# Row buffers, weight buffers and weight transfers of a mixture-of-experts stage rearranged

## The reference

```
def _merge_and_ffn(...):
    x1 = _layernorm(ALPHA * x + mix, ln1_g, ln1_b)
    ffn = _hier_moe(x1, w_group, b_group, w_expert, b_expert, w_gate_up, w_down)
    return _layernorm(ALPHA * x1 + ffn, ln2_g, ln2_b)

for e in range(N_EXPERTS):            # in _hier_moe; gate is zero but for two experts of a token
    gu = xt @ w_gate_up[e]            # 1024 x 512
    h = jax.nn.silu(gu[:, :D_EXPERT]) * gu[:, D_EXPERT:]
    y = y + gate[:, e:e + 1] * (h @ w_down[e])      # 256 x 1024
```

## Time and profile before

| what | value |
|---|---|
| median of three runs | 601.82 us |
| the profiled execution | 602.56 us |
| its span in the trace | 600.9 us |
| PE busy | 518.8 us (86%) |
| DVE, ACT, POOL busy | 373.2, 191.4, 134.0 us |
| DMA from 360 to 560 us | busy all the time, 396 to 419 GB/s |
| chain that ended last | PE 56%, DMA 26%, DVE 8%, ACT 7% |
| largest single item of the chain | loads of gate/up to arena_o, 19% |

### The profile page before, as it was taken

How to read it: one execution, slowest core, us unless ns; L and a number is a source line. 1 busy time by engine, 2 the same in 40 slices (tenths; PEclk the granted TensorE clock), 3 DMA queues, 4 the chain that set the end, 5 groups by cost and what they waited for, 6 DMA issues and landing times.

```text
span 600.9 us, 8960 instructions
## 1 busy us (share of the span) xinstructions
PE 518.8 (86%) x3296; PEld 281.0 (47%) x3296; DVE 373.2 (62%) x722; ACT 191.4 (32%) x356; POOL 134.0 (22%) x156
## 2 busy tenths in 40 slices
PE   5999999999979879899999898888887777767761
PEld 4887788874355443445556743333332222222220
DVE  1642059898933576652258666677886477666686
ACT  0100374214243644121142122444444244432340
POOL 1001054500025760000000201233323222221231
PEclk9999999999979999999999899999999899999997
DMA  9940008570606932001978599999999999999951
GB/s 302 405 155 6 1 1 331 213 269 1 279 5 230 395 116 87 2 1 59 417 290 342 180 420 406 409 396 419 415 415 411 419 418 419 415 415 418 401 193 43
DMA packets 34010, 157.95 MB, mean 263 GB/s; under 512 B 12680, under 2 KB 12680, under 8 KB 20016
## 3 DMA queue, kind: packets, MB, share of 16 engines
q1 hardware_dynamic: 20592, 127.46, 52.9%
q0 software_dynamic: 10752, 29.59, 13.0%
q10 hardware_dynamic: 2624, 0.34, 0.4%
HBM read 160.12 MB, written 21.23 MB: 302 GB/s over the span
## 4 chain that ended last, share of the span: by engine, by line
PE 56%; DMA 26%; DVE 8%; ACT 7%; issue 3%; SPq 0%; POOL 0%; DVEq 0%; POOLq 0%; ACTq 0%
DMA arena_o<-in_w_gu 19%; PE ps L489 17%; PE ps L748 8%; PE ps L962 8%; PE ps L985 4%; PE ps L651 3%; PE ps L589 2%; PE ps L635 2%; DVE arena_s L1477 2%; PE ps L672 2%; DMA first_rows<-arena_s,known 1%; DMA x_rows<-arena_s 1%; PE ps L555 1%; DMA known<-slot_table 1%; DMA slot_table<-arena_s 1%
## 5 line engine op out<-in xcount | busy, mean ns | idle before, releaser
L962 PE MATMUL ps<-arena_w,arena_s 128*64 128x512 f32 x368 | 109.2, 605 | 24.1 <-DMA arena_w<-in_w_gu 12.3
L489 PE MATMUL ps<-arena_w 128*128 128x260 f32 x416 | 94.5, 388 | 6.7 <-DMA arena_w<-in_w_in 6.2
L489 PEld LDWEIGHTS ps<-arena_w 128*128 128x128 f32 x416 | 79.7, 193 | 21.0 <-DMA arena_w<-in_w_in 6.2
L962 PEld LDWEIGHTS ps<-arena_w,arena_s 128*64 128x64 f32 x368 | 33.2, 139 | 96.9 <-issue 66.4
L985 PE MATMUL ps<-arena_w,cs 128*64 128x512 f32 x184 | 56.1, 615 | 20.8 <-ACT cs L1260 20.8
L748 PE MATMUL ps<-arena_o,arena_s 128*128 128x512 f32 x128 | 58.3, 601 | 1.6 <-DVE arena_s L1601 1.6
L962 PE MATMUL ps<-arena_o,arena_s 128*64 128x512 f32 x112 | 50.2, 595 | 0.0
L1477 DVE STREAM_TRANSPOSE arena_s<-arena_w 128x1024 f32<-128x1024 f32 x36 | 41.8, 1214 | 8.3 <-PE ps L589 8.2
L2150 POOL DMA_INDIRECT first_rows<-arena_s,known x15 | 18.0, 1202 | 113.9 <-ACT arena_s L1267 105.1
L1910 DVE TENSOR_TENSOR arena_s<-arena_s,ps 128x256 f32<-128x256 f32 x16 | 6.7, 421 | 56.5 <-ACT arena_s L1256 56.5
L985 PEld LDWEIGHTS ps<-arena_w,cs 128*64 128x64 f32 x184 | 16.0, 141 | 51.0 <-issue 30.3
(11 more groups left out here) (349 smaller groups left out, 897.3 us busy)
## 6 DMA issues: line engine op xcount, KB each, us to landing
arena_w<-in_w_gu SPq DMA_DIRECT2D x46, 1024.0 KB, 19.9
arena_w<-in_w_dn SPq DMA_DIRECT2D x23, 1024.0 KB, 19.9
arena_o<-in_w_gu SPq DMA_DIRECT2D x14, 1024.0 KB, 23.2
arena_o<-in_w_dn SPq DMA_DIRECT2D x7, 1024.0 KB, 23.8
arena_w<-in_w_in SPq DMA_DIRECT2D x13, 512.0 KB, 14.1
arena_o<-in_w_out SPq DMA_DIRECT2D x1, 4096.0 KB, 13.5
arena_s<-in_w_gu SPq DMA_DIRECT2D x4, 1024.0 KB, 8.1
arena_w<-in_xT SPq DMA_DIRECT2D x4, 520.0 KB, 6.7
```

The source lines that it names most:

```text
L489: last = mm(ps[rows, b + n, 0:HALF], lhs(k), rhs(k)[:, n * HALF:(n + 1) * HALF], start=(k == 0), stop=(k == ks - 1))
L962: last = mm(ps[64 * e:64 * e + 64, 2 + q, :], xgT[:, k, CAP * e:CAP * (e + 1)], gu_w[2 * slots + e][:, k, :], start=(k == 0), stop=(k == K ...
```

## The change

Five things change, none of them in the arithmetic but for a clamp.

The gate/up weights lie in another order in memory: both experts' first halves are one block of 2 MB, both second halves another. One transfer of 16 KB per partition takes the place of two of 8 KB per partition. A block fills one slot, so the second half of pair 2 goes to slot 4 and can be issued before the wait for the rows of pair 0.

After pair 2 the two slots in `arena_s` stay weight buffers. The pairs use three buffers in the order 0, 1, 2, 0, 1, 0, 1, 2 and again, so that pairs 8 and 9 wait for the pair two before, and others for the pair three or more before.

The room comes from the rows: `xg` is a ring of four, and the last pass of `finish` writes to `yo[n % 2]`, from where `scatter_out` sends it. So `gather_other(n)` waits until the output of pair n-2 has landed, and `gather_rows` fetches pair n+3, after `scatter_out(n-1)`.

`finish` runs one pair behind instead of two, on DVE, ACT (`root`) and POOL. The end of the program is rewritten: the last pair's own part is added after its partner's, straight from the results of PE, and five small multiplications stand between PE's `products` and `experts` of pair 15.

`residual` multiplies by weights that one pass has multiplied by ALPHA before, and clamps the rows; it has two passes as before.

```diff
+BUFFER = (0, 1, 2, 0, 1, 0, 1, 2)
+GU_SLOT = [[0, 1], [2, 3], [5, 4]]
-S_XG = [5120, 6144, 0, D, S_RT] + [S_SLOT + D * n for n in range(3)]
-S_YO = [S_SLOT + 3 * D, 2 * D, S_SLOT + 4 * D]
+S_XG = [5120, 6144, 0, D]
+S_YO = [S_RT, 2 * D]
...
+def pair_buffer(n):
+
+    return n if n < HEAD else BUFFER[(n - HEAD) % BODY]
+
+
+def before_in(n):
+
+    d = 1
+    while BUFFER[(n - HEAD - d) % BODY] != pair_buffer(n):
+        d += 1
+    return d
...
-            return n % BODY
+            return n % 4
...
+            def gate_up(q, half, pr):
+                sp.dma_start(gu_flat[GU_SLOT[q][half]], w_gu[half, pr].rearrange("o p n -> p (o n)")).then_inc(gu_landed[half][q], 16)
...
             sp.wait_ge(o_done, 16)
-            for half in range(2):
-                gate_up(3, slice(3, 4), half)
+            gate_up(1, 1, slice(1, 2))
             down(3, slice(3, 4))
             store_x1(4)
+            gate_up(2, 1, slice(2, 3))
             landed(sp, x1_stored, TT)
             landed(sp, gathered[0])
-            for half in range(2):
-                gate_up(4, slice(4, 5), half)
             down(4, slice(4, 5))
...
+            def refill(it, n):
+
+                q, used = pair_buffer(n), nth(it, n, add=1 - before_in(n))
+                p = n if it is None or isinstance(it, tuple) else (it * BODY + n) % NPAIR
                 for half, done in enumerate((gu_half, gu_ps)):
                     sp.wait_ge(done, used)
...
+                    gate_up(q, half, slice(p, p + 1) if isinstance(p, int) else bass.ds(p, 1))
...
+                else:
+                    for _ in range(5):
+                        mm(ps[:, 7, 0:P], ident[:, :], ident[:, :], start=True, stop=True)
...
-            finish((past,), NPAIR - 3)
+            finish((past,), NPAIR - 2)
             hidden((past,), NPAIR - 1)
-            finish((past,), NPAIR - 2)
-            own_part((past,), NPAIR - 1, True)
-            finish((past,), NPAIR - 1)
+            finish((past,), NPAIR - 1, True)
...
                 pool.wait_ge(known_landed, there)
+                if n >= 2:
+                    pool.wait_ge(out_landed, gone)
                 pool.wait_ge(scattered[(n - 1) % 2], before)
...
             def pair_step(it, n):
 
-                scatter_own(it, n)
-                if n >= 3:
-                    outs, = number(nth(it, n - 2, 1, 16))
-                    fixed()
-                    pool.wait_ge(out_landed, outs)
-                if n >= 2:
-                    scatter_out(it, n - 2)
                 if n >= 1:
                     gather_other(it, n)
...
+                scatter_own(it, n)
+                if n >= 1:
+                    scatter_out(it, n - 1)
+                    m = n + 3
```

More of the change, by code:

```diff
@@ L119, in nth, with weights_landed @@
     return v if it is None else it * (BODY // per * by) + v
+def pair_buffer(n):
[5 more added lines that the diff above has]
+    return d
+def weights_landed(it, n, unit):
+    if n < HEAD:
+        return unit
+    m, q = n - HEAD, pair_buffer(n)
+    per = BUFFER.count(q)
+    v = unit * (2 + m // BODY * per + BUFFER[:m % BODY].count(q))
+    return it[0] * (unit // 8 * per) + v if isinstance(it, tuple) else it * (unit * per) + v
 def hymba_step(nc, xT, x_tok, kv_cache, rope_cache, conv_st, rec_st, page_rep, lane, w_in, w_kpe, w_uq, w_uk,
@@ L417, in _ @@
             for half in range(2):
-                for j in (0, 1):
-                    gate_up(j, slice(j, j + 1), half)
+                gate_up(0, half, slice(0, 1))
             for j in (0, 1):
                 down(j, slice(j, j + 1))
-            for half in range(2):
-                gate_up(2, slice(2, 3), half)
+            gate_up(1, 0, slice(1, 2))
             down(2, slice(2, 3))
@@ L427, in _ @@
             sp.wait_ge(dec_mixed, 1)
-            for half in range(2):
-                gate_up(5, slice(5, 6), half)
+            gate_up(2, 0, slice(2, 3))
             down(5, slice(5, 6))
@@ L457, in _ @@
             past = sp.value_load(rounds[0:1, 1:2], min_val=0, max_val=(MAXR - 1) * NPAIR)
-            with sp.Fori(0, n_rounds * (NE // 4) - 3) as it:
-                refill(0, (it * 4 + 10) % NE, it * 2 + 4)
-                refill(1, (it * 4 + 12) % NE, it * 2 + 5)
-            refill(0, NE - 2, past + (NPAIR - 2))
+            with sp.Fori(0, n_rounds * 2 - 1) as it:
+                for n in range(HEAD + 2, HEAD + 2 + BODY):
+                    refill(it, n)
+            for n in range(HEAD + 2 + BODY, NPAIR):
+                refill((past,), n)
             landed(sp, outs_stored, 6)
@@ L1914, in residual, with own_part @@
                 x = xg[ring(n)]
[L1915 removed]
+                stt(x, x, ROW_MAX, lng[:, 0, :], ALU.min, ALU.mult).then_inc(residual_step, 1)
                 dve.wait_ge(residual_step, nth(it, n, 1, 2, 1))
[L1917 to L1919 removed]
+                stt(x, x, -ROW_MAX * ROW_MAX, lng[:, 1, :], ALU.max, ALU.add).then_inc(residual_step, 1)
+            def own_part(it, n):
                 x, g = xg[ring(n)], known[:, n // QUAD % 2, 2, n % QUAD:n % QUAD + 1]
@@ L1963, in pair_step @@
                     own_part(it, 0)
-                if n >= 2:
-                    finish(it, n - 2)
+                if n >= 1:
+                    finish(it, n - 1)
                 own_part(it, n)
@@ L2163, in scatter_out @@
-            def scatter_out(it, n):
-                ready, = number(nth(it, n, add=1))
+                                     bounds_check=limit, oob_is_err=False).then_inc(yo_landed[n % 2], 16)
+            def scatter_out(it, n, ready=None, before=None):
+                if ready is None:
+                    ready, before = number(nth(it, n, add=1), nth(it, n, 1, 16))
                 fixed()
+                if n > 0:
+                    pool.wait_ge(out_landed, before)
                 pool.wait_ge(out_ready, ready)
@@ new lines, in pair_step @@
+                if n >= 1:
+                    scatter_out(it, n - 1)
+                    m = n + 3
+                    if n < HEAD:
+                        gather_rows(m, first_at[:, m:m + 1])
+                    elif not isinstance(it, tuple) or m < NPAIR:
+                        there, = number(nth(it, m, QUAD, 16))
+                        fixed()
+                        pool.wait_ge(rows_at_landed, there)
+                        gather_rows(m, rows_at.bitcast(I32)[:, m // QUAD % 2, m % QUAD:m % QUAD + 1])
@@ L2215, in _ @@
                 pair_step((past,), n)
-            n = NPAIR - 1
-            gather_other((past,), n)
-            for k in range(3):
-                scatter_out((past,), n - 2 + k)
-            fixed()
-            landed(pool, out_landed, n_rounds * NPAIR)
+            gather_other((past,), NPAIR - 1)
+            scatter_out((past,), NPAIR - 2)
+            ready, before, stored = number(nth((past,), NPAIR - 1, add=1), nth((past,), NPAIR - 1, 1, 16), n_rounds * (16 * NPAIR))
+            scatter_out((past,), NPAIR - 1, ready, before)
+            pool.wait_ge(out_landed, stored)
 def _lay_out(i):
```

95 lines of the change are left out of this document (38 added, 57 removed).

## The result

The changed kernel takes 629.48 us (median, 628.26 to 630.71) against 602.32 for the kernel before on the same chip: ratio 1.044, 95% interval 1.0414 to 1.0466. The forecast was 600.3, its range ended at 607.5: wrong in sign and far outside. The profiled execution has a span of 627.1 us against 600.9.

A forecast was written before the change was run, and what follows sets the result against it. The prediction took weight bytes through the DMA engines to bound the stage. Head start -5.05, pair 0's gather +0.7, rate 0, dry queue +1 and tail +1.8 sum to -1.55 from 601.82: 600.3 us, range 595.0 to 607.5.

The forecast's parts named there:

- Finishing in the partner's buffer closes a loop over two pairs ... 24.8 us: Steady state: gather_other, finish and scatter_out loop, 28.8 us with +2 each, hidden by the weights' 34.0 for two pairs.
- +2 us for each row transfer: Rows crossing beside 16 KB weight pieces: each transfer takes 2 us longer, bounds 0 and 4.8.
- the estimate of 3.2 us: Row transfers beside gate/up: by the packet-by-packet queue rule, 3.2 us added to each; time about 603.
- PE is 10.4 us late: Early pairs: POOL's new order delays pair 4's rows and hidden(4), leaving PE 10.4 us late from then on.
- I take +1: Weight queue running dry near 440 us, as pair 8's first load waits for pair 6: +1 us, range 0 to 5.
- Head start, -5.05: Last 2 MB of pair 2's gate/up fill the DMA hole from 335 to 340 us; everything behind moves up 5.05 us.
- +0.7 predicted: Gather of pair 0's rows, sharing time with the 2 MB issued earlier: 0.7 us longer, between 0 and 2.3.
- A deeper set of weight buffers cannot make it shorter: Weight stage from 400 to 565 us: bound by bytes, as the buffers before already keep the transfers going.
- Pieces of 16 KB, rate 0: Weight stream in half as many, larger pieces: no change of rate, 0 us, between -2.3 and +2.3.
- Tail +1.8: Kernel end: hidden(15), queued behind finish(14), comes at 586.9 instead of 582.25; end at 598.2 against 596.4, +1.8 us.
- Second rival: Row loop through POOL's queue decides: each row transfer 4.8 us more, loop 34.4 against 34.0, 607.6 us; chance 25%.

The follow-up runs named there:

- f_yo4_two_buffers: Changed kernel (16 KB pieces) with two pairs of weight buffers and four buffers instead of two for partner's and finished rows: 621.34 us, 1.031.
- g_own_first: f_yo4_two_buffers with scatter_own(n) issued ahead of gather_other(n) instead of behind it: 622.16 us, 1.0306.
- c_before_16kb: Kernel before, its order, ring and two pairs of weight buffers kept, with gate/up weights alone in 2 MB transfers of 16 KB per partition: 608.25 us, 1.0089.
- k_one_transfer: Changed kernel, 2 MB gate/up transfers whole, but the two experts' parts apart in DRAM, so a partition's 16 KB comes as two 8 KB pieces: 614.66 us, 1.0162.
- n_early_no_head: Changed kernel, 8 KB pieces, scatter_out(0) and gather_rows(4) ahead of gather_other(1), pair 2's second gate/up block issued behind the waits again: 607.96 us, 1.0084.
- e_two_buffers: Changed kernel with two pairs of weight buffers in the steady state, the third used for pair 2 alone: 629.27 us, 1.0437.
- a_8kb: Changed kernel with each 2 MB gate/up block in two transfers of 8 KB per partition: 608.66 us, 1.009.
- q_no_loop_8kb: g_own_first (two pairs of weight buffers, four row buffers, scatter_own first) in pieces of 8 KB: 610.36 us, 1.0122.
- x_hidden_first: q_no_loop_8kb with hidden(15) ahead of finish(14) on DVE and ACT, as in the kernel before: 603.87 us, 1.001.

## Why the prediction was wrong, point by point

*The failed step: "Finishing in the partner's buffer closes a loop over two pairs ... 24.8 us".* Three things in it failed. It is not over two pairs: POOL's one queue puts scatter_out(n-1) 2.6 us behind gather_other(n), and gather_other(n+1) waits for it: 2.6 + 14.6 + about 1 = 18.2 for each pair, and 16.8 to 18.8 was seen. I had added the data dependences and not followed the queue. For the first eight pairs it had to be compared not with 34.0 for two pairs, but with PE's own 13.4 a pair. And it is one of several: behind it stood the loop of scatter_own, and with both opened some 18 of the 27 us were still lost at 16 KB (f_yo4_two_buffers, g_own_first); what then holds PE, by its waits the ring of four rows and finish one pair behind, is read from one trace and stays open as a cause.

*The term "+2 us for each row transfer", between 0 and +4.8.* Measured +6.5 for out_y (8.1 to 14.6), +6.9 for x_rows (11.3 to 18.2), +0.7 for gather_other at the head of the convoy: for the first two beyond the upper bound, which rested on the one idea that what loads cost doubles. The convoy alone gives out_y 11.3 against 8.1 (at 8 KB), the pieces alone 15.8 against 8.1 (c_before_16kb), both 14.6: they do not add up, and no run says why. Long landings and the new order together are the loss: 21 us of 27 go with 8 KB, and all of it with 4 KB. The rule of the Trainium skill that I cited (DMA: Bandwidth & Descriptors, Queues, rings and completion order), one packet of each queue in turn, would have given the estimate of 3.2 us, half of what out_y showed; the runs agree with its kind, since landings follow the length of the pieces at equal bytes and, in k_one_transfer, at equal transfer size.

*"PE is 10.4 us late"*: already at pair 4's rows, where 8 was worked out, 408.91 against 392.22 is 16.7. Of the 9 beyond the forecast, 6 are the issue of their gather (391.39 instead of 385.3; POOL's first scatter_own already went at 377.60 instead of 372.44) and 2.5 its landing (17.5 instead of 15). *"I take +1"* for the dry queue near 440: 15 us from 400 to 455, since PE was late at every pair and not once.

*Head start, -5.05.* It took place (share 1.05 from 335 to 340), and pair 0's gather paid 0.4 (4.69 instead of 4.32; +0.7 predicted). I did not ask what the buffers do with weights that come early: -1.8 in the kernel before, nothing in the time at 8 KB (n_early_no_head). At 16 KB it was not taken out by itself. *"A deeper set of weight buffers cannot make it shorter"* held for the time in the two runs that took the third pair out, at 16 KB (e_two_buffers) and at 8 KB.

*Pieces of 16 KB, rate 0:* 419 against 416 GB/s, right within its bounds. *Tail +1.8:* the mechanism was named, and in the changed kernel the tail is 2.0 longer (17.6 against 15.6). That agreement is partly luck, since everything there came 24 us later than in the kernel before, and down took 6.1 us instead of 4.3. Where the weights come on time it is dearer: 4 us in a_8kb, 6.5 by experiment between q_no_loop_8kb and x_hidden_first. *Second rival:* its place was right and its price far too small: it too counted 34.4 against 34.0.

Left open: the cause of the 13 us (by the ratios) between g_own_first at 16 KB (622.2) and c_before_16kb (608.3). The tail has no part in them (19.7 against 20.9); by PE's waits (x_rows 22.0 us against 0.7) the ring of four has a large one, but a ring of eight beside four buffers of rows was not run.

## What to carry to other kernels

Follow an in-order queue issue by issue before adding up a loop: a transfer that the next round waits for belongs first in its round, and the loop is to be compared with the pace of the fastest stretch, not with the average one. Longer pieces in a bulk stream are paid by every small transfer beside it, here 3 to 4 us for each doubling in the changed kernel, and 0.6 and then 7.7 us in the kernel before, while the stream gains 2% from 4 to 8 KB and under 1% from 8 to 16; look first whether anything waits for the small ones. Loading earlier is worth something only if a buffer is free for what then follows. And before taking a steady state apart, compare when the last large piece of work ends in both traces: it tells at once whether a loss stands in the stream or in the tail.

## What the runs showed of the hardware

At 4, 8 and 16 KB per partition the weights flow at 406, 416 and 419 GB/s, and a row scatter (out_y) beside them lands in 7.5, 11.3 and 14.6 us in the changed kernel, in 7.5, 8.1 and 15.8 us in the kernel before; the rate is nearly flat where the landing time doubles. Four row transfers issued 1.3 us apart land in 10.2, 12.8, 14.6 and 18.2 us in the order of issue at 16 KB. With order and buffers the same, one transfer of 2 MB in pieces of 8 KB behaves as two of 1 MB for the rows (11.7 against 11.3 us). Waits of PE cost twice: about its wait of 13.59 us, which ended at 408.91, the granted clock was 0.50 from 405 to 415 us, 1.2 GHz, and the pair's down products took 6.04 us instead of 3.65, as they did in the last pair of the changed kernel's chain:

```profile
594.44 3.67 PE ps L1004 x16
610.74 6.14 PE ps L1004 x16
```
